# One decoder layer on one core: the last expert, the slot search, the gather of the expert rows and the final norm rearranged

## The chip, the cores and the metric

The kernel runs on 1 core of one Trainium2 chip. The metric is device microseconds of one execution, given as the median of several runs. "us" is microseconds. The engines are TensorE (PE; its weight loads PEld), VectorE (DVE), ScalarE (ACT), GpSimd (POOL) and SyncE (SP), which here only issues DMAs.

## The reference, cut to what matters

520 tokens (512 prompt, 8 sample) go through a token mixer, then through a mixture of experts and a second norm. Only the last two matter here:

```python
h = layer_norm(ALPHA * x + m, ln1_g, ln1_b)
probs = softmax(h @ router_w + router_b)          # 16 experts in 4 groups of 4
# best group by the sum of its two largest; these two experts are the token's picks
gates = one_hot(sel_i, 16) weighted with sel_v / sum(sel_v)
for e in range(16):
    u = silu(t @ w_gate[e]) * (t @ w_up[e])
    out = out + gates[:, e:e+1] * (u @ w_down[e])
y = layer_norm(ALPHA * h + out, ln2_g, ln2_b)     # D = 1024
```

Both picks of a token lie in one group, and no expert gets over 96 of the 520 tokens in these inputs; the kernel holds a branch with further passes for inputs where one does.

## The kernel before, in words

**Experts.** Each expert gets its tokens as one tile of up to C = 96 rows. A token's row number inside its expert ("pos") comes from the router stage. For each expert POOL gathers 96 rows of h from HBM (`hs`), TensorE turns them, and three products follow: gate and up (96x512 each) and down (96x1024). Every product is done in three matmuls per piece (high weight part x high input, low weight x high input, high weight x low input). The weights of one matrix are 4 chunks of 128x1024. ScalarE writes a chunk's rounded high part into one of 6 places of `ring` (L720); VectorE subtracts it from the weights to get the low part, in place (L1369); of `gate`, the fourth chunk is subtracted by POOL (L544).

**Order of the work.** It is written out by hand. `each_tile` runs `step(e, m, ..)` for expert 0, a loop of two times six experts, and then experts 13, 14 and 15 unrolled. TensorE's step m: gate product of expert m, find_ids, turn u of expert m-1 (L1000), turn the tokens of expert m+1 (L972), up product of m, down product of m-1 (L988 is the matmul line of all products). VectorE's step m, in this order: low parts of up(m), the one-hot of m+2 (up to m = 13), low parts 0 and 1 of down(m-1), `u_low` of m-1 (L1384), `tokens_low` of m+1 (L1375), low parts 2 and 3 of down(m-1), low parts 0 and 1 of gate(m+1), `gated_product` of m (u = silu x up, L1380), low part 2 of gate(m+1). ScalarE ends each step with `rows_out` of m-1: PSUM `work[1]` to `y_out` (L752), which SP stores into `y_rows` in HBM (L409); a next `rows_out` waits for the store.

After step 15, down(15) is still to do: TensorE turns u of expert 15; ScalarE does `rows_out` of expert 14, then the four ring chunks of down(15) and u_hi (L747); VectorE subtracts four chunks, then `u_low`; then TensorE's down product.

**Tail.** VectorE computes for each token the row of `y_rows` of either pick, `slot_a` (first pick) and `slot_b` (second) (L1428 to L1437: 16 instructions for each). Each engine reads the largest count of tokens and branches (`further_passes`, `If`). SP reads `h_back` (the h rows) and `ln2_rows` (g and b of the norm, spread over the partitions), stores the rows of expert 15, waits for all stores and sets `y_read`. POOL then gathers, for 5 blocks of up to 128 tokens, y_a[b] and y_b[b] (L579), ten indirect DMAs. For each block VectorE does `combine` (y_a = y_a * w1 + h_back, L1460; y_a = y_b * w2 + y_a, L1461; two bn_stats L1463, an aggregate L1465, reciprocal L1467, shift L1468), ScalarE takes the root (L806) and writes fin = y_a * scale + bias (L808), POOL multiplies by g (L587), VectorE adds b (L1473), SP stores (L482). `do` issues an instruction that counts a semaphore, `settle` waits for the last one, `step` is both.

## Time and profile before

| | us |
|---|---|
| median of 3 runs | 1136.05 (1134.68 to 1136.72) |
| the profiled execution | 1136.68 |
| its span | 1134.9 |
| TensorE busy | 1004.2 (88%) |
| VectorE busy | 773.2 (68%) |
| ScalarE busy | 502.4 (44%) |
| POOL busy | 406.5 (36%) |
| mean TensorE clock granted | 0.947 |

The span is what the profile covers; the time of the execution is a little longer. Busy shares are averages over stages with different limits. Times in timelines and chains are us from the span's start; the start of one instruction may lie a little before the end of the one before it on the same engine, since they overlap. A name in brackets behind `<-` is what ended the idle time before the instruction. "issue" is time in which an engine waited for nothing that the profile shows. PEclk is the TensorE clock that was granted, 1.00 for 2.4 GHz, 0.50 for 1.2 GHz.

### The profile page before, as it was taken

The page shows a single profiled execution, that of the slowest core. Times are in us where ns is not written, and L with a number is a line of the kernel's source. Part 1 is how long each engine was busy: PE and PEld are TensorE (multiplying, and loading weights), DVE is VectorE, ACT ScalarE, POOL GpSimd, SP SyncE. Part 2 cuts the span into 40 slices and gives each one's busy share as a digit, 9 for nine tenths or more (in the row PEclk, how much of TensorE's full clock was granted, in tenths as well). Part 3 has the DMA queues.
Part 4 walks back from the last instruction along what each step waited for, and adds up shares of the span by engine and source line. Part 5 has one row for each costly group of instructions (what it writes and reads, how often), then busy time and mean ns, then how long its engine had stood idle before and what let it go on. Part 6 is the DMA issues. An engine that isn't in the chain of part 4 may idle for free.

```text
span 1134.9 us, 19648 instructions
## 1 busy us (share of the span) xinstructions
PE 1004.2 (88%) x7141; PEld 904.0 (80%) x7141; DVE 773.2 (68%) x936; ACT 502.4 (44%) x685; POOL 406.5 (36%) x289
## 2 busy tenths in 40 slices
PE   1899999999999899999999989865899999999710
PEld 1899999999999799999999979834677777777500
DVE  0548898888988986744344442464898888988647
ACT  0432333332322144235432222362888787887511
POOL 0344444444444341444554444202212222122053
PEclk9799999999999899999999999986999999999865
DMA  7123333223332221332333347744999999995351
GB/s 195 56 84 103 90 91 89 87 88 92 92 92 74 74 84 52 120 95 83 93 92 92 92 137 233 279 179 147 321 373 382 379 387 382 391 389 220 119 198 66
DMA packets 169491, 189.85 MB, mean 167 GB/s; under 512 B 5827, under 2 KB 121539, under 8 KB 169436
## 3 DMA queue, kind: packets, MB, share of 16 engines
q1 hardware_dynamic: 162600, 176.24, 45.9%
q0 software_dynamic: 3008, 10.55, 2.9%
q10 hardware_dynamic: 3844, 2.57, 1.0%
q8 instruction: 20, 0.33, 0.1%
q14 instruction: 19, 0.16, 0.0%
HBM read 178.57 MB, written 11.76 MB: 168 GB/s over the span
## 4 chain that ended last, share of the span: by engine, by line
PE 83%; DVE 9%; ACTq 2%; ACT 2%; issue 2%; DMA 1%; POOL 0%; POOLq 0%; DVEq 0%; SPq 0%
PE pr L855 54%; PE pr L988 15%; PE work L988 8%; DVE acc_a L1173 1%; ACTq L607 1%; PE work L972 1%; DVE y_a L1461 1%; PE work L926 1%; DVE acc_b L1173 1%; PE work L935 1%; PE work L912 1%; DMA hs<-h_rows,ids 1%; PE pr L1000 1%; DVE v L1185 0%; DVE v L1181 0%
## 5 line engine op out<-in xcount | busy, mean ns | idle before, releaser
L509 POOL TENSOR_TENSOR w_lo<-raw,w_hi 128x512 fp32r<-128x512 f32 x224 | 309.1, 1400 | 380.4 <-ACT w_hi L619 380.4
L855 PE MATMUL pr<-x_hi,w_hi 128*128 128x260 f32 x1280 | 258.9, 283 | 0.0
L855 PE MATMUL pr<-x_hi,w_lo 128*128 128x260 f32 x1280 | 258.4, 284 | 0.0
L855 PE MATMUL pr<-x_lo,w_hi 128*128 128x260 f32 x1280 | 258.0, 283 | 0.0
L623 ACT ACTIVATE ev<-pr 128x520 f32<-128x520 f32 x104 | 63.0, 605 | 419.7 <-PE pr L855 419.7
L855 PEld LDWEIGHTS pr<-x_hi,w_hi 128*128 128x128 f32 x1280 | 198.4, 189 | 0.3
L855 PEld LDWEIGHTS pr<-x_hi,w_lo 128*128 128x128 f32 x1280 | 197.8, 189 | 0.0
L855 PEld LDWEIGHTS pr<-x_lo,w_hi 128*128 128x128 f32 x1280 | 197.3, 189 | 0.0
L1140 DVE SCALAR_TENSOR_TENSOR work<-b_pad,par,work 128x512 f32<-128x512 f32 x224 | 148.2, 748 | 0.0
L619 ACT ACTIVATE w_hi<-raw 128x512 fp32r<-128x512 f32 x224 | 128.0, 623 | 2.2 <-issue 2.0
L988 PE MATMUL pr<-ring,hs_hi 128*96 128x512 f32 x256 | 103.0, 403 | 3.7 <-DVE hs_lo L1375 2.0
L1369 DVE TENSOR_TENSOR w_up_lo<-w_up,ring 128x1024 fp32r<-128x1024 f32 x64 | 77.5, 1254 | 41.0 <-ACT ring L720 41.0
L988 PE MATMUL pr<-ring,hs_lo 128*96 128x512 f32 x256 | 101.5, 397 | 0.0
L544 POOL TENSOR_TENSOR w_gate_lo<-w_gate,ring 128x1024 fp32r<-128x1024 f32 x16 | 51.2, 3200 | 101.1 <-ACT ring L720 101.1
L1369 DVE TENSOR_TENSOR w_down_lo<-w_down,ring 128x1024 fp32r<-128x1024 f32 x64 | 75.1, 1215 | 6.8 <-ACT ring L720 6.8
L1195 DVE TENSOR_TENSOR ev<-ev,ev 128x520 f32<-128x520 f32 x16 | 11.2, 700 | 100.0 <-ACT ev L623 100.0
L720 ACT ACTIVATE ring<-w_gate 128x1024 fp32r<-128x1024 f32 x64 | 67.4, 1061 | 21.9 <-PE pr L988 12.3
L537 POOL DMA_INDIRECT hs<-h_rows,ids x16 | 17.7, 1108 | 152.4 <-DVE ids L1362 136.7
L720 ACT ACTIVATE ring<-w_down 128x1024 fp32r<-128x1024 f32 x64 | 65.6, 1053 | 4.5 <-PE pr L988 4.5
L720 ACT ACTIVATE ring<-w_up 128x1024 fp32r<-128x1024 f32 x64 | 62.4, 1046 | 3.5 <-PE pr L988 3.5
L988 PEld LDWEIGHTS pr<-ring,hs_hi 128*96 128x96 f32 x256 | 41.9, 164 | 22.2 <-DVE hs_lo L1375 2.3
L1369 DVE TENSOR_TENSOR w_gate_lo<-w_gate,ring 128x1024 fp32r<-128x1024 f32 x48 | 57.0, 1214 | 3.6 <-ACT ring L720 3.5
(233 smaller groups left out, 1707.2 us busy)
## 6 DMA issues: line engine op xcount, KB each, us to landing
raw<-in_w_in_dram SPq DMA_DIRECT2D x80, 512.0 KB, 3.7
w_gate<-in_expert_w_gate_dram SPq DMA_DIRECT2D x16, 2048.0 KB, 14.6
w_up<-in_expert_w_up_dram SPq DMA_DIRECT2D x16, 2048.0 KB, 14.1
w_down<-in_expert_w_down_dram SPq DMA_DIRECT2D x16, 2048.0 KB
y_rows<-y_out SPq DMA_DIRECT2D x16, 384.0 KB
raw<-in_w_a_out_dram SPq DMA_DIRECT2D x8, 512.0 KB, 3.6
raw<-in_w_c_out_dram SPq DMA_DIRECT2D x8, 512.0 KB, 3.6
raw<-in_w_b_out_dram SPq DMA_DIRECT2D x8, 512.0 KB, 3.6
```

What stands on the lines that cost most here:

```text
L509: pool.tensor_tensor(w_lo[:, slot, k], raw[:, slot, k], w_hi[:, slot, k].bitcast(F32), ALU.subtract).then_inc(w_split, 1)
L537: pool.indirect_dma_start(out=hs[:], out_offset=None, in_=h_rows, in_offset=bass.IndirectOffsetOnAxis(ap=ids[:, m % 2:m % 2 + 1], axis=0)) ...
L544: pool.tensor_tensor(chunk(kind, s, i, w_e_lo), chunk(kind, s, i), rounded(kind, i, last).bitcast(F32), ALU.subtract).then_inc(ps.lo_pool[ ...
L607: act.dma_start(bs[:], b_spatial[0].partition_broadcast(P)).then_inc(spatial_in, 16)
L619: act.activation(w_hi[:, slot, k], raw[:, slot, k], ACT.Copy).then_inc(w_rounded, 1)
L623: act.activation(out, src[:, :, 0:HALF], func).then_inc(evacuated, 1)
L720: act.activation(rounded(kind, i, last), chunk(kind, s, i), ACT.Copy).then_inc(ps.hi[kind], 1)
L855: mm = pe.matmul(pr[slot][:, h, 0:HALF], w[:, slot, k, :], x[:, k, h * HALF:(h + 1) * HALF], start=(k == 0 and w is w_hi and x is hi), sto ...
L988: mm = pe.matmul(out(h), x[:, k, :], w[:, cols], start=(k == 0 and x is hi and w is w_hi_i), stop=(k == k_of * CH - 1 and x is lo))
L1140: do(dve.scalar_tensor_tensor(acc, b_pad[:, k:k + TP], col(j, R_CONVB + k), acc, ALU.mult, ALU.add))
L1173: do(dve.tensor_reduce(out[:], z[:].rearrange("p k t -> p t k"), AX.X, ALU.add), to(summed))
L1369: dve.tensor_tensor(chunk(kind, s, i, w_e_lo), chunk(kind, s, i), rounded(kind, i, last).bitcast(F32), ALU.subtract).then_inc(ps.lo_dve[ki ...
```

## The change

Four things.

1. **Last expert.** down(14) is no longer part of TensorE's step 15 but follows it in two halves, with the turn of u of expert 15 between them; down(15) follows, from its own tiles `u_hi_last` and `u_lo_last` into PSUM `work[0]`. ScalarE writes ring chunks 0 and 1 of down(15), u_hi_last, chunks 2 and 3, and only then does `rows_out` of experts 14 and 15. VectorE's `u_low_last` stands between low parts 0, 1 and 2, 3.
2. **Slots.** `find_slots` runs on VectorE at the end of step 13 for the first pick and at the end of step 14 for the second, followed by `order_slots`, which puts the lower of the two rows in `slot_a` with its weight `s_wa` and the higher in `slot_b` with `s_wb`, and a copy of the lower, clipped to the rows of experts 0 to 14, in `slot_early`.
3. **Gather.** POOL gathers y_a by `slot_early` as soon as the store of expert 14 has landed, before its branch; y_b after `y_read`. VectorE adds y_a * s_wa + h_back for all blocks (`partials`) as y_a lands. SP issues h_back in step 15 and ln2_rows behind the store of expert 14.
4. **Norm.** ScalarE only takes the root. VectorE computes (y_a - mean) * g and then that * scale + b, each one scalar_tensor_tensor; POOL does nothing in it. The result is stored from y_a.

h_back moves to the place of y_b, y_b to that of h_back, `fin` is gone.

```diff
# SP
                 def step(e, m, third):
...
+                    if m == E - 1 and ps is first:
+                        sp.wait_ge(ps.done["down"], (E - 1) * CH)
+                        load_back()
...
             expert_pass(first, 0, 0)
+            load_rows()
             n_max = further_passes(sp)
...
             with sp.Else():
-                load_back()
                 store(first, E - 1, E - 1, 0)
# POOL
-            def finish(table):
...
+            def fetch(dst, slot, landed, table):
                 for b in range(NTB):
                     n = P if b < 4 else TS
-                    pool.wait_ge(normed, b + 1)
-                    pool.tensor_tensor(fin[0:n, b, :], fin[0:n, b, :], ln2_rows[0:n, 0, :], ALU.mult).then_inc(fin_g, 1)
+                    pool.indirect_dma_start(out=dst[0:n, b, :], out_offset=None, in_=table,
+                                            in_offset=bass.IndirectOffsetOnAxis(ap=slot[0:n, b:b + 1], axis=0)).then_inc(landed[b], 16)
+            pool.wait_ge(slots_ready, 3)
+            pool.wait_ge(first.stored, 16 * E)
+            fetch(y_a, slot_early, y_a_in, y_rows[0:(E - 1) * C, :])
             n_max = further_passes(pool)
...
             with pool.Else():
-                finish(y_rows[0:E * C, :])
+                pool.wait_ge(y_read, 1)
+                fetch(y_b, slot_b, y_b_in, y_rows[0:E * C, :])
# ScalarE
                 each_tile(act, step)
-                rounded_parts(ps, "down", 0, uses[0] + 5, n0 + (E - 1), last=True)
-                u_in(ps, n0 + (E - 1))
-                rows_out(ps, n0 + (E - 1))
+                t = n0 + (E - 1)
+                rounded_parts(ps, "down", 0, uses[0] + 5, t, last=True, chunks=(0, 1))
+                u_in_last(ps, t)
+                rounded_parts(ps, "down", 0, uses[0] + 5, t, last=True, chunks=(2, 3))
+                rows_out(ps, t - 1)
+                rows_out(ps, t, work[0])
...
-                act.wait_ge(scale_ready, b + 1)
-                act.activation(fin[0:n, b, :], y_a[0:n, b, :], ACT.Identity, scale=agg[0:n, s, 2:3],
-                               bias=agg[0:n, s, 3:4]).then_inc(normed, 1)
# TensorE
                 each_tile(pe, step)
-                turn_u(ps, n0 + (E - 1))
-                down(ps, 0, n0 + (E - 1), last=True)
+                t = n0 + (E - 1)
+                down(ps, (E - 2) % 3, t - 1, chunks=(0, 1))
+                turn_u(ps, t)
+                down(ps, (E - 2) % 3, t - 1, chunks=(2, 3))
+                down_last(ps, t)
# VectorE
                     if m < 15:
                         low_parts(ps, "gate", (m + 1) % 3, t + 1, (2, 3))
+                    if ps is first and m == 13:
+                        find_slots(oh1, s_slot)
+                    if ps is first and m == 14:
+                        find_slots(oh2, s_slot2)
+                        order_slots()
                 each_tile(dve, step)
-                low_parts(ps, "down", 0, n0 + (E - 1), last=True)
-                u_low(ps, n0 + (E - 1))
+                t = n0 + (E - 1)
+                low_parts(ps, "down", 0, t, (0, 1), last=True)
+                u_low_last(ps, t)
+                low_parts(ps, "down", 0, t, (2, 3), last=True)
+
+            def find_slots(oh, out):
+                do(dve.tensor_tensor(t2[:], oh[:], e_off[:], ALU.mult))
+                do(dve.tensor_tensor(probs[:], oh[:], pos[:], ALU.mult))
+                settle()
+                do(dve.tensor_reduce(out[:], t2[:], AX.X, ALU.add))
+                step(dve.tensor_reduce(s_ps[:], probs[:], AX.X, ALU.add))
+                step(dve.tensor_tensor(out[:], out[:], s_ps[:], ALU.add))
+                for k in range(1, PASSES):
+                    step(dve.tensor_scalar(s_t[:], s_ps[:], float(k * C), float(E * C - C), ALU.is_ge, ALU.mult))
+                    step(dve.tensor_tensor(out[:], out[:], s_t[:], ALU.add))
+
+            def order_slots():
+                step(dve.tensor_tensor(s_t[:], s_slot[:], s_slot2[:], ALU.is_gt))
+                do(dve.tensor_tensor(s_wa[:], s_w2[:], s_t[:], ALU.mult))
+                do(dve.tensor_tensor(s_wb[:], s_w1[:], s_t[:], ALU.mult))
+                step(dve.tensor_scalar(s_t[:], s_t[:], -1.0, 1.0, ALU.mult, ALU.add))
+                do(dve.tensor_tensor(s_w1[:], s_w1[:], s_t[:], ALU.mult))
+                step(dve.tensor_tensor(s_w2[:], s_w2[:], s_t[:], ALU.mult))
+                do(dve.tensor_tensor(s_wa[:], s_wa[:], s_w1[:], ALU.add))
+                do(dve.tensor_tensor(s_wb[:], s_wb[:], s_w2[:], ALU.add))
+                do(dve.tensor_tensor(s_t[:], s_slot[:], s_slot2[:], ALU.min))
+                step(dve.tensor_tensor(s_ps[:], s_slot[:], s_slot2[:], ALU.max))
+                do(dve.tensor_copy(slot_a[:], s_t[:]), to_slots)
+                do(dve.tensor_copy(slot_b[:], s_ps[:]), to_slots)
+                step(dve.tensor_scalar(s_t[:], s_t[:], float((E - 1) * C - 1), None, ALU.min))
+                step(dve.tensor_copy(slot_early[:], s_t[:]), to_slots)
+
+            def partials(landed):
+                for b in range(NTB):
...
+                    dve.wait_ge(y_a_in[b], landed)
+                    dve.scalar_tensor_tensor(a, a, s_wa[0:n, b:b + 1], h_back[0:n, b, :], ALU.mult, ALU.add).then_inc(partial_ready, 1)
...
+            def summed_up(b):
+                dve.wait_ge(y_b_in[b], 16)
+                dve.wait_ge(partial_ready, NTB)
+                step(dve.scalar_tensor_tensor(y_a[0:n, b, :], y_b[0:n, b, :], s_wb[0:n, b:b + 1], y_a[0:n, b, :], ALU.mult, ALU.add))
...
+                do(dve.bn_aggr(agg[0:n, s, 0:2], stats[0:n, s].rearrange("p h c -> p (h c)")), to_var)
+
+            def normalise(b):
+                n, s = P if b < 4 else TS, b % 2
+                to_var.wait(0 if b == NTB - 1 else 1)
+                do(dve.scalar_tensor_tensor(y_b[0:n, b, :], y_a[0:n, b, :], agg[0:n, s, 0:1], ln2_rows[0:n, 0, :], ALU.subtract, ALU.mult))
+                dve.wait_ge(std2_ready, b + 1)
+                do(dve.reciprocal(agg[0:n, s, 2:3], agg[0:n, s, 2:3]))
+                settle()
+                do(dve.scalar_tensor_tensor(y_a[0:n, b, :], y_b[0:n, b, :], agg[0:n, s, 2:3], ln2_rows[0:n, 1, :], ALU.mult, ALU.add), to_fin)
...
+            summed_up(0)
+            for b in range(1, NTB):
+                summed_up(b)
+                normalise(b - 1)
+            normalise(NTB - 1)
```

## Rows read from the trace of the kernel before

**Rows 1.** The page's head: span, then busy us, share and instructions of TensorE and others.
```profile
span 1134.9 us, 19648 instructions
PE 1004.2 (88%) x7141; PEld 904.0 (80%) x7141; DVE 773.2 (68%) x936; ACT 502.4 (44%) x685; POOL 406.5 (36%) x289
```

**Rows 2.** The chain of waits: start, us, what ran.
```profile
1055.72 5.56 PE pr L988 x24
...
1061.29 5.57 PE work L988 x24
...
1074.02 8.46 PE work L988 x24
...
1083.55 3.27 DMA y_rows<-y_out
...
1088.56 5.44 DMA y_b<-y_rows,slot_b
```

**Rows 3.** Groups by line, 1094 to 1135: count | busy, mean ns | idle before.
```profile
L1463 DVE BATCH_NORM_STATS2 stats<-y_a 128x6 f32<-128x512 f32 (+1 forms) x10 | 6.4, 683 | 0.2
...
L1465 DVE BATCH_NORM_AGGREGATE agg<-stats 128x2 f32<-128x12 f32 (+1 forms) x5 | 1.0, 206 | 0.2
```

**Rows 4.** VectorE's timeline in the norm: start, us, instruction, [idle before].
```profile
1095.42 1.28 DVE L1461 SCALAR_TENSOR_TENSOR y_a<-y_b,s,y_a 128x1024 f32<-128x1024 f32 x1
...
1106.32 3.24 DVE L1461 SCALAR_TENSOR_TENSOR y_a<-y_b,s,y_a 128x1024 f32<-128x1024 f32 x1
...
1131.49 1.21 DVE L1473 TENSOR_TENSOR fin<-fin,ln_rows 8x1024 f32<-8x1024 f32 x1 [2.58 <-POOL fin L587]
```

**Rows 5.** VectorE's timeline: two router instructions, first and fifteenth of a slot search.
```profile
765.33 0.16 DVE L1334 TENSOR_TENSOR g<-g,g 128x20 f32<-128x20 f32 x1
765.42 0.16 DVE L1335 TENSOR_TENSOR g<-g,g 128x20 f32<-128x20 f32 x1
...
1073.88 0.23 DVE L1428 TENSOR_TENSOR router<-router,e_off 128x80 f32<-128x80 f32 x1
...
1076.74 0.17 DVE L1436 TENSOR_TENSOR s<-s,s 128x5 f32<-128x5 f32 x1
```

**Rows 6.** VectorE's timeline, steps 14 and 15.
```profile
1034.62 4.63 DVE L1369 TENSOR_TENSOR w_up_lo<-w_up,ring 128x1024 fp32r<-128x1024 f32 x4 [2.96 <-ACT ring L720]
...
1047.91 1.22 DVE L1369 TENSOR_TENSOR w_gate_lo<-w_gate,ring 128x1024 fp32r<-128x1024 f32 x1
1051.87 4.63 DVE L1369 TENSOR_TENSOR w_up_lo<-w_up,ring 128x1024 fp32r<-128x1024 f32 x4 [2.75 <-ACT ring L720]
```

**Rows 7.** POOL's timeline.
```profile
770.41 4.03 POOL L537 DMA_INDIRECT hs<-h_rows,ids  x1 [22.43 <-DVE ids L1362]
...
1030.62 3.32 POOL L544 TENSOR_TENSOR w_gate_lo<-w_gate,ring 128x1024 fp32r<-128x1024 f32 x1 [4.82 <-ACT ring L720]
1048.25 3.14 POOL L544 TENSOR_TENSOR w_gate_lo<-w_gate,ring 128x1024 fp32r<-128x1024 f32 x1 [14.31 <-ACT ring L720]
1087.29 0.96 POOL L579 DMA_INDIRECT y_a<-y_rows,slot_a  x1 [35.90 <-SPq L476]
...
1094.77 1.43 POOL L579 DMA_INDIRECT y_a<-y_rows,slot_a  x1 [0.31 <-issue]
...
1105.30 3.18 POOL L587 TENSOR_TENSOR fin<-fin,ln_rows 128x1024 f32<-128x1024 f32 x1 [1.50 <-ACT fin L808]
```

**Rows 8.** Timelines of POOL and of VectorE in step 1.
```profile
798.86 3.26 POOL L544 TENSOR_TENSOR w_gate_lo<-w_gate,ring 128x1024 fp32r<-128x1024 f32 x1 [6.93 <-ACT ring L720]
...
799.79 4.55 DVE L1369 TENSOR_TENSOR w_up_lo<-w_up,ring 128x1024 fp32r<-128x1024 f32 x2
```

**Rows 9.** Windows: length, busy of PE, PEld, DVE, ACT, POOL, then PEclk, DMA share, GB/s.
```profile
796.00:806.00 10.00, 7.29 (x39) 4.66 (x40) 9.90 (x9) 9.28 (x11) 3.26 (x1) 1.00 0.90 301
...
1069.50:1070.00 0.50, 0.00 (x0) 0.00 (x0) 0.50 (x1) 0.50 (x2) 0.00 (x0) 0.64 0.88 303
...
1074.00:1079.50 5.50, 5.48 (x13) 3.73 (x14) 4.71 (x28) 0.00 (x0) 0.00 (x0) 0.50 1.02 386
```

**Rows 10.** ScalarE's timeline behind the last copy of y_out.
```profile
1086.18 1.28 ACT L806 ACT_TABLE_LOAD   x1 [2.66 <-issue]
```

More of the change, by code:

```diff
@@ L190, in build @@
         y_a = place("y_a", "X_HI", [P, NTB, D])
-        y_b = place("y_b", "X_HI", [P, NTB, D], plus=NTB * D * 4)
-        fin = place("fin", "Q_HI", [P, NTB, D], plus=(NTB + 2) * D * 4)
-        h_back = place("h_back", "Q_HI", [P, NTB, D])
+        h_back = place("h_back", "X_HI", [P, NTB, D], plus=NTB * D * 4)
+        y_b = place("y_b", "Q_HI", [P, NTB, D])
         ln2_rows = place("ln2_rows", "Q_HI", [P, 2, D], plus=NTB * D * 4)
@@ L240, in build @@
         u_hi = place("u_hi", "ev4", [P, FB, C], F32R, plus=C * 4)
+        u_hi_last = place("u_hi_last", "ev0", [P, FB, C], F32R)
+        u_lo_last = place("u_lo_last", "bs", [P, FB, C], F32R)
         u_lo = place("u_lo", "par", [P, FB, C], F32R)
@@ L592, in _ @@
                     expert_pass(further, q * E)
-                finish(y_rows)
+                pool.wait_ge(y_read, 1)
+                fetch(y_a, slot_a, y_a_in, y_rows)
+                fetch(y_b, slot_b, y_b_in, y_rows)
             with pool.Else():
-                finish(y_rows[0:E * C, :])
+                pool.wait_ge(y_read, 1)
+                fetch(y_b, slot_b, y_b_in, y_rows[0:E * C, :])
         @block.scalar
@@ L973, in turn, with product @@
                 mm.then_inc(ps.turned, 1)
-            def product(ps, kind, s, t, hi, lo, out, halves, last=False):
+            def product(ps, kind, s, t, hi, lo, out, halves, last=False, chunks=range(CH)):
                 k_of = CW // (halves * 512)
-                for i in range(CH):
+                for i in chunks:
                     by_pool = i in BY_POOL[kind]
@@ L990, in product, with down, down_last @@
                     mm.then_inc(ps.done[kind], 1)
-            def down(ps, s, t, last=False):
+            def down(ps, s, t, chunks=range(CH)):
+                if 0 in chunks:
+                    pe.wait_ge(ps.u_lo_ready, t + 1)
+                    pe.wait_ge(ps.y_ready, t + 1)
+                product(ps, "down", s, t, u_hi, u_lo, lambda h: work[1][0:C, h, :], 2, chunks=chunks)
+            def down_last(ps, t):
                 pe.wait_ge(ps.u_lo_ready, t + 1)
-                pe.wait_ge(ps.y_ready, t + 1)
-                product(ps, "down", s, t, u_hi, u_lo, lambda h: work[1][0:C, h, :], 2, last)
+                product(ps, "down", 0, t, u_hi_last, u_lo_last, lambda h: work[0][0:C, h, :], 2, last=True)
             def turn_u(ps, t):
@@ L1380, in gated_product, with u_low_last @@
                 dve.tensor_tensor(u[:], silu[:], pr[0][0:C, 1, :], ALU.mult).then_inc(ps.u_ready, 1)
+            def u_low_last(ps, t):
+                dve.wait_ge(ps.u_hi_ready, t + 1)
+                dve.tensor_tensor(u_lo_last[:].rearrange("p f t -> p (f t)"), pr[1][:, 0, 0:FB * C],
+                                  u_hi_last[:].rearrange("p f t -> p (f t)").bitcast(F32), ALU.subtract).then_inc(ps.u_lo_ready, 1)
             def u_low(ps, t):
@@ L1422, in _ @@
+            def partials(landed):
+                last[0] = chain
+                for b in range(NTB):
+                    n = P if b < 4 else TS
+                    dve.wait_ge(y_a_in[b], landed)
+                    a = y_a[0:n, b, :]
+                    dve.scalar_tensor_tensor(a, a, s_wa[0:n, b:b + 1], h_back[0:n, b, :], ALU.mult, ALU.add).then_inc(partial_ready, 1)
             dve.sem_inc(first.ids_ready, 1)
@@ L1446, in _ @@
                     expert_pass(further, q * E)
-                dve.nop()
+                dve.wait_ge(back_in, 128)
+                partials(32)
             with dve.Else():
-                dve.nop()
-            dve.wait_ge(back_in, 64)
-            def combine(b):
+                dve.wait_ge(back_in, 64)
+                partials(16)
+            def summed_up(b):
                 n, s = P if b < 4 else TS, b % 2
-                dve.wait_ge(y_in[b], 32)
-                if b >= 2:
-                    dve.wait_ge(normed, b - 1)
-                a = y_a[0:n, b, :]
-                step(dve.scalar_tensor_tensor(a, a, s_w1[0:n, b:b + 1], h_back[0:n, b, :], ALU.mult, ALU.add))
-                step(dve.scalar_tensor_tensor(a, y_b[0:n, b, :], s_w2[0:n, b:b + 1], a, ALU.mult, ALU.add))
+                dve.wait_ge(y_b_in[b], 16)
+                dve.wait_ge(partial_ready, NTB)
+                step(dve.scalar_tensor_tensor(y_a[0:n, b, :], y_b[0:n, b, :], s_wb[0:n, b:b + 1], y_a[0:n, b, :], ALU.mult, ALU.add))
                 for h in range(2):
```

70 lines of the change are left out of this document (24 added, 46 removed).

## The prediction

> **What bounds the kernel now.** I read the page's head first [rows 1], where TensorE is busy 88% of the span: it bounds everything up to the last expert, and a change that touches nothing before step 13 can gain only at its end. The chain of waits over the last 85 us [rows 2] shows four parts there. Until 1066.87 it is matmuls, 5.56 us a product. Then comes the last expert's own chain of 7.1 us, in which TensorE stands: y_out copied, ring written, four low parts subtracted, u_lo; and then a down product of 8.46 us where its predecessor took 5.57. Third, copy, store and ten gathers (1082.5 to 1094.0). Fourth, the norm on VectorE, from 1094.10 to the end of its last row at 1132.70 [rows 4]; the span ends 2.2 us later with the last output transfer. The change touches the last three, and puts small instructions under the first.
>
> **Norm (1094.10 to 1132.70, 38.6 us).** Before, each block is two scalar_tensor_tensor (STT), two bn_stats, one aggregate on VectorE, then ScalarE, a POOL multiply and a VectorE add. The second STT takes 1.28 in blocks 0 and 1 and 3.24 in blocks 2 to 4 (one row of each kind in [rows 4]): that of block 2 is issued at 1106.32, behind POOL's multiply (1105.30 to 1108.48) [rows 7], and ends 1.1 us after it. After the change POOL multiplies nothing; the first STT moves to `partials`, early. A steady block then holds, start to start: STT 1.32 (1095.42 to the bn_stats at 1096.74 of the same chain, [rows 4]), two bn_stats of 0.68 less their overlap, 1.33 [rows 3], the aggregate 0.14 (0.21 [rows 3] less the 0.07 by which instructions that don't wait for each other overlap, as those of 0.16 at 0.09 in [rows 5]), subtract-and-scale STT 1.22, reciprocal 0.20 (the step of a small instruction with its wait, [rows 5]), last STT 1.21 = 5.4 us. The square root of ScalarE (0.29) has a whole block to hide in. Sum: `summed_up(0)` 2.8 + 4 x 5.4 + the last `normalise` 2.8 = 27.3 us, against 38.6: 11.3 saved. The new STT form (subtract, mult, with a row of ln2) stands in no row; the same engine, shape and number of operands gives 1.28, an addition of two tensors 1.21 [rows 4], and I take 1.28. Its bounds are 1.2 and the 3.24 of the slow rows.
>
> **Slots in steps 13 and 14.** `find_slots` is 15 of the 16 instructions of the old code: 1073.88 to 1076.93, 3.05 us [rows 5]. VectorE idles 2.96 us at the end of step 13 and 2.75 at the end of step 14 [rows 6], so by durations the first is covered. But that idle time is exactly when POOL subtracts the gate weights' fourth chunk (1030.62 to 1033.94) [rows 7]. [rows 8] show what happens when VectorE issues a tensor_tensor behind such a POOL instruction: the chunk issued at 799.79 finished at 803.2 in place of 801.0, 1.1 after POOL's 802.12. `find_slots` begins with a tensor_tensor of two SBUF tensors, so I let it wait until 1033.94; it ends at 1036.9 and w_up_lo of expert 14 starts 2.3 us late. Bounds: 0.05 (no block) and 2.3. TensorE's needs follow back from 1055.72 (`up` of expert 15, [rows 2]) by 5.56 a product, 0.33 a turn of u: down(13) begins at 1044.3, `up` of expert 14 at 1038.7. Its first low chunk is there at 1038.1; four up chunks, two down chunks (1.14 each) and u_lo (0.5) from 1036.9 give 1044.3 to 1044.4, which costs it 0.1. The Trainium skill, "SBUF — State Buffer", section "Who interferes with whom", says the same of the pair: a VectorE instruction with two SBUF inputs contends with a GpSimd instruction that reads SBUF, and whoever is first keeps the port for the whole instruction. The rows agree with it (3.4 us in place of 1.2) [rows 8]. By the rule the delay is 2.3 us and the time the forecast below; without it the delay is 0.05 and the time that of rival (a).
>
> In step 14 the late VectorE has its gate subtractions still to do when POOL's next one is issued at 1048.25. One of them waits for it, and the third ends at about 1053.1 instead of 1049.13. Then `find_slots` 3.05 and `order_slots`: 6 instructions with a wait at 0.20 (15 in 3.05) and 8 without at 0.09 (765.33 to 765.42) = 1.95 [rows 5]. VectorE is free at 1058.0; it used to start w_up_lo(15) at 1051.87. Its first chunk is ready at 1059.2 (1.21); TensorE stands at `up` of expert 15 from 1055.8: **a stall of 3.4 us**. From there both run in step (VectorE 1.14 a chunk, TensorE 1.39): `up` ends at 1064.8 instead of 1061.29. Two down chunks (2.3) and u_lo (0.5) hold down(14) until 1065.4; its first half lasts until 1068.2; `gated_product` ends at 1068.3 behind two more chunks; turning u takes 0.33; the second half ends at 1071.4, against 1066.87.
>
> **The last expert without its chain.** ScalarE writes ring chunks 0 and 1 as soon as `up` is done and u_hi_last right behind the turn, VectorE subtracts them during down(14): low parts 0 and 1 by 1070.6, u_lo_last by 1071.0, both before 1071.4. So down(15) starts at once and takes 5.57: the 8.46 stood in a stretch at granted 0.50, the 1.2 GHz level, behind 7 us of idle [rows 9], and that idle goes. It ends at 1077.0, against 1082.48: 5.5 saved out of 9.7 that there were to have without the stall (7.1 idle and 2.9 of clock, less 0.33).
>
> **Gathers.** Store(14) follows down(14): copy 1.05 (1082.48 to 1083.55), store 3.3 [rows 2], so 1075.8. POOL reacts in 0.45 (store landed 1086.82, first gather 1087.29 [rows 7]) and issues five y_a gathers 1.25 apart (1087.29, 1088.56): until 1082.4. Then it loads the count and branches, work that used to lie in its idle time. No row shows that on POOL. ScalarE does the same between y_out and its next instruction and needs 2.66 us [rows 10], some of which may not be the branch; the low end is 0, if it costs nothing, and 2.66 the high end. I take 2.0, nearer to the row. Meanwhile down(15), copy and store have set y_read at 1081.4, so POOL, not the store, is last: first y_b gather at 1084.4. Landing takes 5.44 from issue [rows 2], so 1089.8. Partials (five STT of 1.28 as y_a lands, the last about 1087.5) are done by then. h_back, now issued about 1051 behind store(13), would have to take over 30 us to be late; it takes the place of the same issue at 1069.7 and frees nothing on the path. ln2_rows (1 MB) go right behind store(14) on SP and are out of the way before the first gather moves bytes; were they not, store or gather would be 1 to 2 us later.
>
> **Sum.** The norm starts at 1089.8 instead of 1094.1 (4.3) and is 11.3 shorter: 1117.1, + 2.2 = span 1119.3, 15.6 less than 1134.9. The profiled execution took 1136.68, 1.8 above its span; the median of the runs is 1136.05. I take the 15.6 off the median: **1120.5 us**.
>
> **Rivals.**
> (a) *No port wait for the small instructions, slots hidden.* VectorE is then free at 1054.1, the stall disappears but for 0.2 at u_lo; down(15) ends at 1073.1 and store(14) lands at 1071.8: all 4.0 earlier, 1116.5. For: the instructions are of 0.2 us, most with tiny operands. Against: [rows 8].
> (b) *POOL's branch is free.* The y_b gathers start at 1082.85, when POOL is through its y_a gathers, and the time is 1118.9.
> (c) *The clock falls in the stall.* TensorE stopped at 1066.9 and the grant is 0.64 over 1069.50 to 1070.00, so it fell within; it was 0.50 in the first 5.5 us after work resumed [rows 9]. A stall of 3.4 us may do the same. In 5.5 us at half rate 2.8 are lost, and down(14) and its store shift as much: 1123.3. Against: between 796 and 806 TensorE was busy only 7.29 of 10 us and the grant stayed 1.00, though in several short gaps [rows 9]. The Trainium skill, "TensorE: Matmul & The Clock Gate", section "HAM oscillation — how this bites in real kernels", warns of waits between bursts that put the array back to the low clock; by it this case would come out at 1123.3 too.
> (d) *VectorE holds up POOL's descriptors.* One gather issued beside an STT took 1.43 where the first took 0.96, and the first of the expert stage, beside low parts, 4.03 [rows 7]. Partials and y_b gathers now coincide; at worst the first y_b is 3.1 late: 1123.6.
> (e) *Slower: 3.24 us is the price of the STT, not of POOL.* If operands so placed cost 3.24 whatever POOL does, each block has three: 5.4 + 3 x 1.96 = 11.3, the norm about 56.7 us, the time 1150. It decides from a mean STT of about 2.3 us (1.28 and the 15.6 us saved, spread over 15 of them). Against: two blocks at 1.28, with the same tiles.
>
> **How the numbers follow.** Forecast 45%, (a) 17%, (b) 10%, (c) 18%, (d) 7%, (e) 3%. A difference under 0.2% (2.3 us) can't be told from none here. All but (e) lie at least 10 us below 1136: faster 0.96, same 0.01, slower 0.03. Range: (a) with a little of (b) below, (c) or (d) with some late landing above: 1115.0 to 1125.0.
>
> **What would show it.** In the changed trace: the first instruction of `find_slots` in step 13 ends after POOL's w_gate_lo; TensorE idles about 3.4 us before the first w_up_lo matmul of expert 15, granted clock 1.00; down(15) follows down(14) without a gap and takes 5.6; about 2 us lie between POOL's fifth y_a and first y_b gather; the STTs are 1.28 and blocks 5.4 apart. It is wrong if VectorE starts w_up_lo(15) before 1056, if down(15) is again at half rate, or if the norm is over 30 us long.

## The result, and the profile after

The changed kernel takes 1121.55 us (median of 4 runs, 1120.17 to 1121.61), the kernel before, run beside it, 1135.55 us: a ratio of 0.9873, 95% interval 0.9860 to 0.9885. The prediction was 1120.5 us with a range of 1115.0 to 1125.0. The page's head after; it answers [rows 1]:

```profile
span 1119.8 us, 19649 instructions
PE 1003.7 (90%) x7141; PEld 903.5 (81%) x7141; DVE 777.0 (69%) x948; ACT 496.8 (44%) x680; POOL 393.2 (35%) x284
```

The busy times are those of before within 1.5%, but for POOL's 13.3 us less; the span is 15.1 us shorter. So the time came out of waits, those of VectorE for the port among them, which the page counts as busy time. The chain of waits after, from step 14 on; it answers [rows 2]:

```profile
1049.91 2.77 DVE w_gate_lo L1386
...
1057.47 1.24 DVE w_up_lo L1386
1058.75 7.36 PE pr L997 x24
1066.11 2.78 PE work L997 x12
1068.89 0.33 PE pr L1014 x4
1069.22 2.79 PE work L997 x12
1072.03 1.04 ACT y_out L761
1073.09 2.98 DMA y_rows<-y_out
...
1079.40 7.69 DMA y_a<-y_rows,slot_early
1087.11 1.28 DVE y_a L1487
1088.41 2.48 DVE y_a L1487 x2
1090.98 1.30 DVE y_a L1513
```

Two things stand in it that were not in the chain before: VectorE (its slot instructions fill 1052.67 to 1057.45) ahead of `up` of expert 15, which takes 7.36 us in place of 5.56; and, at the end, a low gather's landing of 7.69 us with three partial sums behind it, in place of a high gather's landing. (The low gathers are those of y_a, issued early; the high ones are those of y_b; a partial sum is y_a * s_wa + h_back.) The first high gather, issued at 1085.41, landed after 5.5 us, at 1090.9: a tie with the partial sums. In the second profile of the same kernel (y0) the partial sums were last by 1.1 us. POOL's timeline of that stretch; it answers [rows 7]:

```profile
1030.65 3.79 POOL L555 TENSOR_TENSOR w_gate_lo<-w_gate,ring 128x1024 fp32r<-128x1024 f32 x1 [4.64 <-ACT ring L725]
1048.29 3.31 POOL L555 TENSOR_TENSOR w_gate_lo<-w_gate,ring 128x1024 fp32r<-128x1024 f32 x1 [13.84 <-ACT ring L725]
1076.89 0.96 POOL L585 DMA_INDIRECT y_a<-y_rows,slot_early  x1 [25.29 <-DMA y_rows<-y_out]
...
1081.89 0.89 POOL L585 DMA_INDIRECT y_a<-y_rows,slot_early  x1 [0.30 <-issue]
1085.41 1.98 POOL L585 DMA_INDIRECT y_b<-y_rows,slot_b  x1 [2.64 <-SPq L487]
```

SP's waits (us in total, times, the longest); store(15), that of expert 15's rows, took 6.0 us to land:

```profile
SPq L483 <- DMA y_rows<-y_out: 6.0, 1, 6.0
```

And TensorE's first matmul of `up` of expert 15, with 2.67 us of idle time ahead of it:

```profile
1058.75 0.47 PE L997 MATMUL pr<-ring,hs_hi 128*96 128x512 f32 x1 [2.67 <-DVE w_up_lo L1386]
```

To compare kernels, I count from the start of POOL's w_gate_lo in step 13. From there on every kernel runs alike but for its edits; the stages ahead of it scatter by up to 3.2 us from run to run. Starts in us from that point, each from the timelines of the kernel named (the last column is the norm's length to the end of VectorE's last instruction, with the first STT of block 0 where it lies in the norm):

| kernel | y_out(15) copy | first gather | first y_b gather | norm | norm's length |
|---|---|---|---|---|---|
| before | 51.9 | 56.7 | 57.9 | 63.5 | 38.6 |
| after | 46.9 | 46.2 | 54.8 | 60.3 | 26.5 |
| after, second profile (y0) | 46.6 | 46.3 | 53.5 | 61.1 | 26.5 |
| x1, no POOL part | 43.0 | 42.6 | 48.8 | 57.0 | 26.6 |
| x2, TensorE busy in the stall | 46.0 | 45.7 | 52.5 | 60.5 | 26.5 |
| x3, slots ahead of expert 0 | 42.1 | 41.4 | 49.7 | 56.5 | 26.5 |
| x4, rows early | 46.9 | 46.4 | 53.0 | 60.6 | 26.5 |
| x5, norm of before | 46.8 | 46.6 | 53.1 | 61.4 | 26.4 |
| x6, gathers late | 46.6 | 51.7 | 53.0 | 58.5 | 33.1 |
| x7, old order of last expert | 55.9 | 45.8 | 61.3 | 65.9 | 26.5 |
| x8, x3 and x4 together | 42.1 | 41.5 | 48.7 | 55.1 | 26.6 |
| x9, slot search shortened | 43.8 | 43.5 | 50.4 | 58.2 | 26.5 |
| x10, x8 with partials in turn | 42.1 | 41.5 | 47.8 | 53.5 | 30.7 |

Of the 15.1 us, 3.1 are the norm's earlier start and 12.1 its length. The two profiles of the same changed kernel differ by 0.8 us in the norm's start, so less than that is not read from one profile here.

### The profile page after: what moved, and what is told of

It reads as the page before. It is cut to its first block, busy times and chain, and to the rows that moved or that the text cites. A ratio compares the mean times of both kernels' runs of the same rounds, so it can differ in the third digit from the quotient of the medians.

```text
span 1119.8 us, 19649 instructions
## 1 busy us (share of the span) xinstructions
PE 1003.7 (90%) x7141; PEld 903.5 (81%) x7141; DVE 777.0 (69%) x948; ACT 496.8 (44%) x680; POOL 393.2 (35%) x284
## 3 DMA queue, kind: packets, MB, share of 16 engines
q1 hardware_dynamic: 162600, 176.24, 46.6%
## 4 chain that ended last, share of the span: by engine, by line
PE 79%; DVE 12%; DMA 3%; ACTq 2%; issue 2%; ACT 1%; POOL 0%; SPq 0%; DVEq 0%; POOLq 0%
PE pr L864 55%; PE pr L997 12%; PE work L997 6%; DMA y_rows<-y_out 2%; DVE acc_a L1190 2%; ACTq L612 1%; DVE w_up_lo L1386 1%; PE work L981 1%; DVE w_down_lo L1386 1%; PE work L935 1%; DVE w_gate_lo L1386 1%; DVE acc_b L1190 1%; DMA y_a<-y_rows,slot_early 1%; PE work L944 1%; PE work L921 1%
## 5 line engine op out<-in xcount | busy, mean ns | idle before, releaser
L725 ACT ACTIVATE ring<-w_down 128x1024 fp32r<-128x1024 f32 x64 | 65.9, 1055 | 10.8 <-PE pr L997 10.6
```

The lines of the kernel that those rows point to most:

```text
L725: act.activation(rounded(kind, i, last), chunk(kind, s, i), ACT.Copy).then_inc(ps.hi[kind], 1)
```

## The experiments

The ratios are to the kernel before, run beside each kernel on the same chip, with 95% intervals. The unaltered changed kernel, run again (y0_after), gave 1122.23 us, 0.9880 (0.9862 to 0.9898). Three chips were used: one for x1 to x4, one for y0 and x5 to x7, one for x8 to x10. So kernels are compared through their ratios, not their times.

> The changed kernel itself, unaltered, as the measure for the others on this chip. All theories: ratio to the kernel before 0.986 to 0.9885, about 15 us less; the span's stretches as in the first trace: stall of 2.7 us ahead of up(15), norm of 26.5 us.

**x1_no_pool_part: who holds up VectorE.** For experts 14 and 15 POOL subtracts 8 columns of its chunk, not 1024, and TensorE reads chunk 2's low part in its place.

```
+                    if isinstance(t, int) and t >= E - 2:
+                        pool.tensor_tensor(chunk(kind, s, i, w_e_lo)[:, 0:8], ...)
...
+                    if by_pool and isinstance(t, int) and t >= E - 2:
+                        w_lo_i = chunk(kind, s, 2, w_e_lo)
```

> The changed kernel, but POOL's subtraction of the gate weights' fourth chunk is cut to 8 columns for experts 14 and 15, and TensorE uses chunk 2's low part in its place (so part of the computation is changed). Theory (port): in the changed kernel one small VectorE instruction of the first slot search took 1.85 us and one low part in step 14 took 2.84 us, both ending as POOL's instruction ended. Without it they take 0.17 and 1.22, w_up_lo of expert 15 starts at about 1054.5 instead of 1057.47, TensorE's idle time of 2.7 us ahead of up(15) goes, the granted clock stays 1.00, the down product of expert 15 ends 4 to 4.5 us earlier and the time is about 4 us shorter. Rival (the 29 small instructions are too long by themselves): the idle time stays at 1.5 us or more and the time moves by under 1.5 us.

Measured 1117.56 us, 0.9843 (0.9826 to 0.9859). VectorE's timeline of the changed kernel, then of x1:

```profile
1032.37 0.23 DVE L1458 TENSOR_REDUCE s<-router 128x5 f32<-128x80 f32 x1
1032.63 1.85 DVE L1459 TENSOR_TENSOR s<-s,s 128x5 f32<-128x5 f32 x1
...
1036.54 4.63 DVE L1386 TENSOR_TENSOR w_up_lo<-w_up,ring 128x1024 fp32r<-128x1024 f32 x4
...
1049.83 2.84 DVE L1386 TENSOR_TENSOR w_gate_lo<-w_gate,ring 128x1024 fp32r<-128x1024 f32 x1
1052.60 0.23 DVE L1454 TENSOR_TENSOR router<-router,e_off 128x80 f32<-128x80 f32 x1
```
```profile
1030.32 0.17 DVE L1465 TENSOR_TENSOR s<-s,s 128x5 f32<-128x5 f32 x1
...
1032.87 3.50 DVE L1392 TENSOR_TENSOR w_up_lo<-w_up,ring 128x1024 fp32r<-128x1024 f32 x3 [0.35 <-ACT ring L729]
...
1046.16 1.21 DVE L1392 TENSOR_TENSOR w_gate_lo<-w_gate,ring 128x1024 fp32r<-128x1024 f32 x1
```

The addition of 128x5 numbers that took 1.85 us takes 0.17, and the gate part of 2.84 takes 1.21. The waits are POOL's doing, and with them goes the stall: TensorE waits 0.4 us, the grant (the granted clock) stays 1.00, y_out(15) is copied 3.6 to 3.9 us earlier. The ratio is 0.0037 below y0's, and its interval lies below y0's. The run also settles POOL's branch, which the stores no longer hide here:

```profile
1075.92 0.89 POOL L589 DMA_INDIRECT y_a<-y_rows,slot_early  x1 [0.30 <-issue]
1077.21 0.95 POOL L589 DMA_INDIRECT y_b<-y_rows,slot_b  x1 [0.40 <-SPq L487]
```

0.40 us lie between the last y_a gather and the first y_b gather, where two gathers of one loop are 0.30 apart. Loading the count and branching cost POOL 0.1 us at most.

**x2_busy_in_stall: the clock.** Ten matmuls into a free PSUM bank ahead of `up` of expert 15; nothing reads them.

```
+                    if m == E - 1 and ps is first:
+                        for _ in range(10):
+                            pe.matmul(work[0][0:C, 0, :], hs_hi[:, 0, 0, :], w_e_lo["gate"][0][:, 0:512], ...)
```

> The changed kernel with ten added 128x512 matmuls (2.3 us, result not used) in TensorE's idle time ahead of up(15). Theory (clock): up(15) took 7.36 us because the grant fell to 0.50 from about 1059.7 to 1063.2; with TensorE busy the grant stays 1.00, up(15) takes 5.6 to 5.8, the down product of expert 15 ends 1.5 to 1.8 us earlier, and the time is 1 to 1.8 us shorter. Rival (up is paced by VectorE's low parts, 1.14 us each, behind the late start): up(15) still takes about 7 us and the time stays.

Measured 1119.61 us, 0.9850 (0.9835 to 0.9865). Windows of the changed kernel over its stall and the product behind it (columns as in [rows 9]), then of x2:

```profile
1057.00:1058.50 1.50, 0.00 (x0) 0.00 (x0) 1.43 (x5) 0.70 (x2) 0.00 (x0) 1.00 1.03 423
1059.00:1059.50 0.50, 0.50 (x3) 0.32 (x2) 0.50 (x1) 0.00 (x0) 0.00 (x0) 1.00 0.24 98
1059.50:1060.00 0.50, 0.50 (x3) 0.41 (x2) 0.50 (x2) 0.00 (x0) 0.00 (x0) 0.75 0.10 41
1060.00:1063.00 3.00, 3.00 (x8) 1.95 (x8) 3.00 (x3) 1.06 (x1) 0.00 (x0) 0.50 0.00 1
1063.00:1063.50 0.50, 0.50 (x3) 0.28 (x3) 0.50 (x2) 0.14 (x1) 0.00 (x0) 0.84 0.00 0
```
```profile
1055.00:1060.00 5.00, 4.64 (x23) 3.08 (x22) 4.55 (x23) 3.35 (x5) 0.00 (x0) 1.00 0.92 366
1060.00:1065.00 5.00, 5.00 (x23) 3.39 (x21) 5.00 (x5) 2.13 (x2) 0.00 (x0) 1.00 0.03 11
```

Here the grant is still 1.00 in the stall and for 1.0 us of work behind it (the row of 0.75 holds both levels, half each); then it is 0.50, the 1.2 GHz level, for 3.4 us: 8 matmuls in 3.0 us, where x2 has 23 in 5.0. In y0 it fell at about 1058.9, within the stall, 0.6 us before work resumed, and again for 3.4 us. With TensorE busy it never drops, though `up` starts as late. The profiles put the clock's price at 1.8 us of `up` (7.36 against 5.56; 7.04 in y0) and at 0.6 to 0.9 at y_out(15), since VectorE's u_lo then holds x2 up by 0.3. Nothing of it is left at the norm in this one profile (60.5 against 60.3 and 61.1), whose fourth low gather took 8.4 us. The ratio is 0.0030 below y0's, 3.4 us, but its interval and y0's overlap: that the clock slowed `up` is shown, what it costs the whole kernel is not.

**x3_slots_early: the slot search out of the expert steps.** Both picks by one set of instructions, in VectorE's 6.4 us of idle time ahead of expert 0's tokens.

```
+            def find_both():
+                for i, oh in enumerate((oh1, oh2)):
...
+                step(dve.tensor_tensor(s_both[:], s_both[:], s_pb[:], ALU.add))
...
                take_ids(ps, 1, n0 + 1)
+                if ps is first:
+                    find_both()
+                    order_slots()
```

> The changed kernel with the slots found before expert 0, where VectorE idled 6.4 us for the first gather of tokens; the two picks share the ten compare-and-add instructions (31 instructions in place of 44, about 5.7 us). Theory: steps 13 to 15 run as before the change, no idle time of TensorE ahead of up(15), grant 1.00, the down product of expert 15 ends 4 to 4.5 us earlier (about 1073), the norm starts as much earlier, the time is 4 us shorter (1117.5). Rival (what ends last is the DMA stretch of gathers and store, which has a rate of its own): the store and gathers start 4 us earlier too but land no faster, so the same 4 us; if instead the first gather of the stage is disturbed by VectorE, expert 0 starts later and less than 3 us is left.

Measured 1117.91 us, 0.9837 (0.9823 to 0.9850), 0.0043 below y0. Chain and VectorE's timeline of x3:

```profile
1049.25 5.56 PE pr L999 x24
...
1055.14 5.56 PE pr L999 x24
```
```profile
1046.94 1.22 DVE L1388 TENSOR_TENSOR w_gate_lo<-w_gate,ring 128x1024 fp32r<-128x1024 f32 x1
1051.29 4.63 DVE L1388 TENSOR_TENSOR w_up_lo<-w_up,ring 128x1024 fp32r<-128x1024 f32 x4 [3.13 <-ACT ring L727]
```

The stall is gone, VectorE idles 3.13 us before the up parts as in [rows 6], and y_out(15) comes 4.5 to 4.8 us earlier: the stall of 2.7 and the clock's 1.8. The 0.0043 are 4.9 us, and the interval lies below y0's. The work was made shorter too (31 instructions for 44, 5.7 us in the trace), so x3 does not show what the place alone is worth; x9 below shortens it and leaves it in the expert steps. Where VectorE idled for another reason it cost next to nothing: the tokens of expert 0 came 0.4 to 0.5 us later behind their gather than in the changed kernel's two profiles, and by step 13 this is lost in the scatter (260.0 us from that gather to POOL's w_gate_lo, 259.9 and 261.6 in the changed kernel's two profiles).

**x4_rows_early: do the row loads slow the store?** `load_rows()` beside `load_back()` in SP's step 15 (issued at 1052), not behind store(14).

```
                         load_back()
+                        load_rows()
...
-            load_rows()
```

> The changed kernel with the two loads of the norm's rows (1 MB in SBUF) issued with h_back at about 1051 instead of behind the store of expert 14. Theory (DMA stretch): the store of expert 15 took 6.35 us to land and the third y_a gather 7.7 us because 1 MB of rows, two stores and 2 MB of gathers shared 1074 to 1087 at 250 to 390 GB/s; without the rows the store lands in 3.5 to 4.5 us, the gathers in 5 to 6, the norm starts about 2 us earlier, the time is 1.5 to 2.5 us shorter. Rival (the y_a gathers alone hold up the store, the rows were through by then): the store still takes about 6 us and the time moves by under 0.7 us.

Measured 1120.32 us, 0.9856 (0.9841 to 0.9871). Store(15) landed after 4.2 us, not 6.0 or 5.1, and the first y_b gather was issued 0.5 to 1.8 us earlier. The norm began where it did (60.6 against 60.3 and 61.1). One such pair does not show that the row loads had slowed the store: with the rows where they were it landed after 4.0 us in x1 and 4.4 in x5, with the rows early after 3.7 in x8. And a store that landed 0.9 to 1.8 us sooner did not matter for the norm: the fourth low gather landed 7.8 us after its issue, at 1087.8, the two partial sums behind it ran until 1090.4, and the first high gather (1082.85, landed after 6.4) was there at 1089.3. POOL's fourth low gather and the start of the norm in x4:

```profile
1080.00 0.94 POOL L585 DMA_INDIRECT y_a<-y_rows,slot_early  x1 [0.30 <-issue]
...
1090.44 1.28 DVE L1513 SCALAR_TENSOR_TENSOR y_a<-y_b,s,y_a 128x1024 f32<-128x1024 f32 x1
```

**x5_old_norm: is it the fused form (subtract and multiply, then multiply and add, in one instruction each)?** The norm of before (ScalarE's scaling, POOL's multiply, VectorE's shift), with only the first STT kept in `partials`.

```
+                pool.wait_ge(normed, b + 1)
+                pool.tensor_tensor(fin[0:n, b, :], fin[0:n, b, :], ln2_rows[0:n, 0, :], ALU.mult).then_inc(fin_g, 1)
...
-                normalise(b - 1)
+                shift(b - 1)
```

> The changed kernel with the norm of before (ScalarE scale and shift, POOL multiply, VectorE add, result in its own tile), only the first STT of each block stays in the early partials. Theory (order of issue decides the port): the STT that took 3.24 us was issued behind POOL's multiply only because another STT stood ahead of it; without that one it is issued right behind the add of the block before, ahead of POOL's multiply, and takes 1.28. Then a block takes about 4.9 us, the end of the last block through ScalarE and POOL about 5, the norm 28 to 29 us in place of 26.5: the time is only 1.5 to 2.5 us longer than the changed kernel's. Rival (POOL's multiply still blocks it, two fused ops are the gain): STT 3.24 in three blocks, block 6.9 us, norm 34 to 36, the time 8 to 10 us longer.

Measured 1121.44 us, 0.9872 (0.9852 to 0.9892). The norm is 26.4 us long, as the fused one, and the ratio does not differ from y0's. VectorE and POOL in x5:

```profile
1100.14 1.28 DVE L1523 SCALAR_TENSOR_TENSOR y_a<-y_b,s,y_a 128x1024 f32<-128x1024 f32 x1
1100.33 3.29 POOL L605 TENSOR_TENSOR fin<-fin,ln_rows 128x1024 f32<-128x1024 f32 x1 [1.37 <-ACT fin L825]
...
1114.42 2.33 POOL L605 TENSOR_TENSOR fin<-fin,ln_rows 8x1024 f32<-8x1024 f32 x1 [1.45 <-ACT fin L825]
1116.79 1.21 DVE L1535 TENSOR_TENSOR fin<-fin,ln_rows 8x1024 f32<-8x1024 f32 x1 [2.55 <-POOL fin L605]
```

With one STT fewer in the block, VectorE issues the other 0.2 us ahead of POOL's multiply instead of 1 us behind it as in [rows 4, 7]. It takes 1.28, and POOL waits. Blocks are 4.68 us apart (the next STT is at 1104.82), shorter than the fused 5.3, but the last block still goes through ScalarE, POOL (2.33) and VectorE.

**x6_gather_late: what the early gather brings.** All ten gathers after y_read as before, both STTs in the block, the fused form kept.

```
+                    for dst, slot, landed in ((y_a, slot_a, y_a_in), (y_b, slot_b, y_b_in)):
...
+                step(dve.scalar_tensor_tensor(y_a[0:n, b, :], y_a[0:n, b, :], s_wa[0:n, b:b + 1], h_back[0:n, b, :], ...))
```

> The changed kernel without the early gather: y_a and y_b are gathered in turns after y_read, and y_a * s_wa + h_back is computed at the head of each block, as before the change. Theory (the early gather brings no earlier start, it only takes five STT off the norm): the store of expert 15 lands in about 4 us in place of 6.35 because no gather is in flight, y_read comes 2 us earlier, y_b of block 0 lands at about the same time as in the changed kernel (within 1.5 us), the norm starts as early but takes 33 us in place of 26.5: the time is 5 to 6.5 us longer. Rival (the early gather also starts the norm earlier, by the five gathers saved): norm starts 4 us or more later as well, the time is 9 us or more longer.

Measured 1125.73 us, 0.9922 (0.9898 to 0.9946), 0.0042 above y0 (the intervals touch; against the first pair's 0.9873 they are apart). x6's marks (VectorE's first STT of block 0, then the second):

```profile
1088.60 1.28 DVE L1514 SCALAR_TENSOR_TENSOR y_a<-y_a,s,h_back 128x1024 f32<-128x1024 f32 x1 [16.35 <-DMA y_b<-y_rows,slot_b]
1089.91 1.28 DVE L1515 SCALAR_TENSOR_TENSOR y_a<-y_b,s,y_a 128x1024 f32<-128x1024 f32 x1
```

Its norm starts 1.9 to 2.6 us **earlier** than that of the changed kernel, and is 6.6 us longer. Store(15) landed after 3.2 us, with no gather beside it. The early gather starts nothing sooner: what it buys is that five STTs run while the gathers land. With x5 this closes a square of norm lengths: both STTs in the block, old form 38.6, fused 33.1; one STT, old form 26.4, fused 26.5. The form alone is worth 5.5 us, the moved STT alone 12.2, both together 12.1, no more than the moved STT.

**x7_old_last: what the reordered last expert brings.** Down(14) whole, then the turn, then down(15), as before; the second u buffers and PSUM bank kept.

```
-                down(ps, (E - 2) % 3, t - 1, chunks=(0, 1))
+                down(ps, (E - 2) % 3, t - 1)
                 turn_u(ps, t)
-                down(ps, (E - 2) % 3, t - 1, chunks=(2, 3))
```

> The changed kernel with the order of before around the last expert: down(14) whole, then turn, y_out(14) ahead of the four ring chunks, the four low parts ahead of u_lo. Theory: TensorE stands 7 us ahead of down(15), the grant falls and down(15) takes about 8.5, its end comes 9.5 to 10 us later; but y_a is gathered meanwhile and the store of expert 15 then lands in 3.5 us in place of 6.35, so the norm starts only 6 to 7 us later and that is the time lost. Rival (nothing is given back): 9.5 us longer or more.

Measured 1126.26 us, 0.9915 (0.9898 to 0.9932), 0.0035 above y0 (the intervals touch). TensorE idles 6.86 us for u_lo_last and y_out(15) comes 9.0 to 9.3 us later, but the norm only 4.8 to 5.5: store(15) lands in 3.5 us with no gather beside it, and the high gather in 4.54. Some 40 to 50% of what the reordering saves is given back in the landings.

**x8_both, x9_slots_shorter, x10_in_turn.** x8 is x3 and x4 together. x9 does both searches in step 13 and leaves only the ordering in step 14. x10 is x8 with the partial sums taken in turn. The core of x9's edit, then of x10's:

```
                     if ps is first and m == 13:
-                        find_slots(oh1, s_slot)
+                        find_both()
                     if ps is first and m == 14:
-                        find_slots(oh2, s_slot2)
                         order_slots()
```
```
+            partial(0)
+            partial(1)
             summed_up(0)
             for b in range(1, NTB):
+                if b < NTB - 1:
+                    partial(b + 1)
                 summed_up(b)
```

> Slots found ahead of expert 0 and the scale and shift rows loaded with h_back at step 14, both together. Theory 1 (between the first low gather and the norm it is the gathers' own landing that ends last, 14.1 to 15.1 us in every run with an early gather so far): the gain of x3_slots_early is kept, ratio to the kernel before 0.983 to 0.985; the store of expert 15 lands in about 4.2 us instead of 5.7, and the norm starts no more than 0.7 us earlier than in x3 for it, at 1085.8 to 1086.5. Rival (the store's landing sets the start, and x3 hid its part of it): the norm starts 1.5 us or more earlier than in x3, by 1085.0, and the ratio is 0.982 or less.

> The slots of both picks are found in step 13 by one set of instructions (17 where the kernel has 2 x 11), and only their ordering stays in step 14: the slot work between the third gate low part and the first up low part of step 14 goes from 4.85 us to about 2.0. Theory 1 (TensorE's stall ahead of up(15) is what this slot work outlasts, and the clock falls because the stall is near 3 us): the stall goes from 2.7 us to 0.4 or less, the clock stays at 1.00 through up(15), which takes 5.6 instead of 7.0 to 7.4, and the ratio is 0.984 to 0.986 against 0.988 of the unaltered kernel. Rival (the slot work of step 13 costs as much when it grows by some 1.5 us there): TensorE waits 1.5 us or more in step 14, and the ratio is 0.987 or more.

> x8_both, with the partial sums taken in turn with the blocks: block 0 of the norm waits only for the first two low gathers and its own high gather, no longer for all five low ones. ScalarE passes each landing on to VectorE. Theory 1 (the wait for all five partial sums starts the norm): in x8 the last low gather lands about as late as the first high one, so the norm starts when the first high gather lands, 0.5 to 2 us earlier than in x8, and each block is as long as before plus its 1.28 us partial sum, 26 to 28 us from start to end; ratio 0.001 below x8 or equal. Rival (the partial sums are covered by nothing once they lie in the norm): the norm grows by five times 1.28 less the part hidden before ScalarE's square root, 4 us or more, and x10 is 0.002 or more above x8.

x8: 1116.07 us, 0.9827 (0.9814 to 0.9841), the fastest. Its interval lies below y0's; against x3 (0.9837) the gain is not resolved in the runs, though the norm starts 1.4 us earlier in the profile. The size lies between the theory's (at most 0.7) and the rival's (1.5 or more), and the rival's mechanism was not it: store(15) landed in 3.7 us, but the first high gather was there at 1082.9, and the norm still waited for the fourth low gather (issued at 1073.95, landed at 1081.1) and the partial sums behind it, until 1083.7. The low gathers took 4.7 to 7.2 us where x3's took 6.8 to 8.7. I read it so that in x3 the 1 MB of rows lay ahead of gathers and store alike; that was not tried by itself, and x4, the same step from the changed kernel, moved neither its low gathers nor its norm by as much.

x9: 1118.56 us, 0.9851 (0.9836 to 0.9866). Slot work between the low parts of step 14 is 1.8 us long, TensorE waits for no up part (0.2 us for a gate part, 0.5 in two for u_lo), the grant is 1.00, y_out(15) 2.8 to 3.1 us earlier than in the changed kernel and 1.7 later than in x3. The ratio fell as the theory said, but its interval and y0's overlap a little. The longer search in step 13 moved POOL's chunk of step 14 by 0.7 us and no more.

x10: 1120.67 us, 0.9867 (0.9852 to 0.9882), 0.0040 above x8. The start of the norm is 1.6 us earlier, as theory 1 says, and the norm 4.1 us longer, as the rival says: each block now carries a partial sum (x10's VectorE in block 1):

```profile
1085.29 1.23 DVE L1490 SCALAR_TENSOR_TENSOR y_a<-y_a,s,h_back 128x1024 f32<-128x1024 f32 x1
1086.63 1.28 DVE L1514 SCALAR_TENSOR_TENSOR y_a<-y_b,s,y_a 128x1024 f32<-128x1024 f32 x1
```

So waiting for all five partial sums is the better order: VectorE has the time before the last landing, and none after it.

## Why the prediction was right, point by point

**Norm.** Predicted 38.6 to 27.3, blocks 5.4; measured 26.5 and 5.3 (1093.75, 1099.01, 1104.32). The STT with subtract and a row of ln2, which had no row, takes 1.24 as the others. The sum was right, its account was not: I ascribed the gain to POOL's multiply going and to the moved STT without parting them. x5 shows that the multiply could have stayed; moving one STT out of the block turned the order in which VectorE and POOL reach the port. Rival (e) is dead: the 15 STTs of the norm average 1.24 to 1.28 us by line.

**Slots in step 13.** Predicted: the search's first instruction waits until POOL is done, w_up_lo(14) starts 2.3 us late. Measured: it starts at 1036.54 (predicted 1036.9), but the first four instructions ran, and the fifth waited. VectorE's own part was first to the port at 1030.66, two tensor_tensors followed it without a gap, and POOL got in only when VectorE came to its tensor_reduces. (x1 agrees: its subtraction of 8 columns, issued at 1028.37, ended at 1029.94, behind VectorE's two tensor_tensors there.) The Trainium skill, "SBUF — State Buffer", section "Who interferes with whom", says that a tensor_reduce never contends here and that a two-input tensor_tensor does; the trace agrees, since both reductions ran at 0.24 and 0.23 us beside POOL and the addition took 1.85. Net, POOL's chunk ended at 1034.44 instead of the 1033.94 that I took.

**Step 14 and the stall.** VectorE free at 1057.45 (predicted 1058.0), stall 2.67 (predicted 3.4). The step held, 0.7 us too long.

**Clock.** The forecast had 1.00, with rival (c) at 18% and 2.8 us. This step failed: the stall took the grant to 0.50 for 3.4 us, and `up` took 1.8 us longer. Rival (c)'s mechanism was there at two thirds of its price. The rest of the chain took most of it up: `up` had started 0.5 us earlier than forecast, and of the 0.6 us that down(14) was to wait for u_lo nothing was left, so down(14) ended at 1072.0, forecast 1071.4. Down(15) followed at once, at the full clock, and took 5.55 (1072.03 to 1077.58, the two copies), as forecast.

**Gathers.** Here the forecast had its path wrong, and two of its terms nearly cancelled. POOL's first low gather came 0.8 us behind store(14)'s landing, where 0.45 were taken, and store(14) landed 0.3 sooner than taken. POOL's branch: 2.0 taken, 0.1 at most measured (x1), so rival (b) was right about the branch. Store(15): I let it land in 3.3 us; among gathers and rows it took 6.0, and it, not POOL, was last before y_b: 1085.4, forecast 1084.4. (It is no fixed figure: 5.1 in y0, 4.0 to 5.7 in the other profiles with the rows behind store(14) and the early gather.) Then the partial sums, forecast done at about 1087.5, ended at 1090.87, as the third and fourth low gather, forecast at 5.44 us like any, took 7.7; the first high gather landed at 1090.9. In y0 and in x1 to x5, x8 and x9 too it was the partial sums that ended last. The norm started at 1090.98, forecast 1089.8.

**Rivals (a) and (d).** (a), slots hidden, was wrong for this kernel and right as a price: x3 makes it true and is worth 4.9 us by the ratios where 4.0 were worked out. (d): the first two y_b gathers took 1.98 and 1.51 on POOL beside STTs, but the first still landed 5.5 us after its issue, so nothing was late for it.

**Sum.** Span 1119.8 against 1119.3: +1.2 at the start of the norm, -0.8 in it, +0.1 behind it. The norm's 11.3 us, the larger part of the forecast, were sized rightly. That its start came within 1.2 us is in part luck: a branch of 2.0 us that is not there stood against a store 2.7 us too short, and a stall 0.7 us too long against a fall of the clock taken at nothing.

**Open.** Why the third and fourth low gathers take 7.7 us and the first 5.9 (4.7 in x8), whether for the bytes ahead of them or for their number, was not separated. Nor was the fused form together with x8 tried against the old one.

## What to carry to other kernels

Work moved into another engine's idle time is not hidden by its duration: look at what the neighbour on the port does in that very stretch, and prefer an idle time that ends on something unrelated (x3, with the work shortened as well, against the change: 4.9 us by the ratios). Where two engines meet at a port once per block, ask which one issues first; taking one 1.3 us instruction out of the block ahead of the meeting saved 12.2 us over five blocks, 6.4 of them its own, and the rewritten arithmetic nothing beyond that. An early transfer that shares the queues with the last store pays only by the computation that it lets run under the landings.

## What the runs showed of the hardware that I had not expected

- POOL's 128x1024 subtraction or multiply takes 2.3 us when it has the port; the 3.1 to 3.8 in the rows hold its wait. From the changed kernel, worked out: it ran from the end of VectorE's second tensor_tensor (about 1032.15) to 1034.44. From x5: 2.33 with VectorE idle, 3.29 beside an STT of 1.28. In x1 8 columns of it still read 1.57 and 1.74.
- An idle time of TensorE of 2.67 us took the grant to 0.50 for 3.4 us. The fall came 0.5 to 1.0 us after work had resumed in the changed kernel and in x4 to x7, but 0.6 before it in y0. With 0.4 us of idle time (x1, x2) the grant stayed at 1.00.
- A store of 384 KB landed in 3.2 us with no gather beside it (x6), in 3.7 to 4.2 beside five gathers (x8, x10, x4), and in 4.0 to 6.0 beside five gathers with 1 MB of row loads issued just ahead of them (x1 to x3, x5, x9 and both profiles of the changed kernel).
- Some gathers issued on POOL beside an STT took 1.5 to 2.0 us in place of 0.94 (the changed kernel's at 1085.41 and 1087.70), others beside one did not (x1's at 1079.72 took 0.93); what decides is not shown. The first gather of the expert stage, issued beside VectorE's subtractions, ended 0.96 us behind the last of them (774.76 against 773.80), and in x3, where two tensor_tensors of the slot search followed at once, 0.96 behind those (774.40 against 773.44).
